# Moving two accumulations of the modulation on the vector engine in a two-block transformer kernel

## The reference, cut to what matters

```python
c_act = jax.nn.silu(c)
mod = (c_act @ w_ada[l] + b_ada[l])[:, None, :]
shift1, scale1, gate1, shift2, scale2, gate2 = jnp.split(mod, 6, axis=-1)
h = rms_norm(x, norm1_w[l]) * (1.0 + scale1) + shift1
proj = h @ w_in[l]
...
A = jnp.where(strict, jnp.einsum('bhncd,bhnsd->bhncs', kb, k) * decay, 0.0)
L = A + jnp.eye(CHUNK, dtype=A.dtype)
sol = lax.linalg.triangular_solve(L, rhs, left_side=True, lower=True, unit_diagonal=True)
qk = jnp.where(causal, jnp.einsum('bhncd,bhnsd->bhncs', q, k) * decay, 0.0)
...
x = x + gate1 * mixed
```

## Time and profile before

| | us |
|---|---|
| median of 3 runs | 953.57 |
| lowest and highest of the runs | 953.0, 954.26 |
| the profiled execution, its own time | 958.16 |
| its span, from the first to the last instruction | 956.1 |
| PE busy in the span | 942.1 (99%) |
| DVE busy | 743.2 (78%) |
| ACT busy | 540.4 (57%) |
| POOL busy | 63.7 (7%) |

### The profile page before, as it was taken

How to read it: one execution, slowest core, us unless ns; L and a number is a source line. 1 busy time by engine, 2 the same in 40 slices (tenths; PEclk the granted TensorE clock), 3 DMA queues, 4 the chain that set the end, 5 groups by cost and what they waited for, 6 DMA issues and landing times.

```text
span 956.1 us, 15251 instructions
## 1 busy us (share of the span) xinstructions
PE 942.1 (99%) x6383; PEld 812.3 (85%) x6383; DVE 743.2 (78%) x841; ACT 540.4 (57%) x687; POOL 63.7 (7%) x60
## 2 busy tenths in 40 slices
PE   8999999999999999999999999999999999999997
PEld 5799888988878788999888888889999888888886
DVE  2699978878887887787669987777776668987874
ACT  3584467466546465634265664657655656655554
POOL 0000660000100000100000000010000000000000
PEclk9999979999999999999999999999999999999999
DMA  9877224766798878556536878778653464978761
GB/s 338 298 255 284 72 84 140 271 219 253 174 354 213 315 182 309 208 181 212 202 115 166 269 214 272 214 212 288 257 170 128 144 218 142 259 217 269 216 176 44
DMA packets 41555, 204.54 MB, mean 214 GB/s; under 512 B 3408, under 2 KB 5904, under 8 KB 25744
## 3 DMA queue, kind: packets, MB, share of 16 engines
q1 hardware_dynamic: 35024, 180.37, 52.0%
q0 software_dynamic: 5760, 22.05, 12.4%
q10 hardware_dynamic: 704, 1.17, 0.4%
HBM read 202.49 MB, written 1.07 MB: 213 GB/s over the span
## 4 chain that ended last, share of the span: by engine, by line
PE 88%; DVE 6%; ACT 2%; DMA 1%; issue 1%; POOL 1%; SPq 0%; DVEq 0%; POOLq 0%; ACTq 0%
PE bank L2179 44%; PE acc L2179 41%; PE bank L2830 2%; DMA X_inv<-stream 1%; DVE w_lo L1419 1%; POOL X_inv L839 1%; PE bank L2576 1%; ACT w_hi L933 0%; DVE scores L1443 0%; DVE XT L1725 0%; PE bank L2281 0%; PE acc L2281 0%; PE bank L2286 0%; PE bank L2453 0%; DVE qkT L1713 0%
## 5 line engine op out<-in xcount | busy, mean ns | idle before, releaser
L1419 DVE TENSOR_TENSOR w_lo<-raw,w_hi 128x2048 fp32r<-128x2048 f32 x125 | 284.5, 2288 | 51.0 <-ACT w_hi L933 50.7
L933 ACT ACTIVATE w_hi<-raw 128x2048 fp32r<-128x2048 f32 x125 | 237.4, 1911 | 66.1 <-PE acc L2179 41.5
L2179 PE MATMUL bank<-w_hi,h_parts 128*128 128x512 f32 x696 | 225.0, 393 | 0.0
L2179 PE MATMUL acc<-h_parts,w_hi 128*128 128x256 f32 x928 | 169.7, 285 | 1.3 <-DVE h_parts L1471 0.7
L2179 PEld LDWEIGHTS bank<-w_hi,h_parts 128*128 128x128 f32 x696 | 130.7, 188 | 29.7 <-DVE h_parts L1496 1.5
L2179 PEld LDWEIGHTS acc<-h_parts,w_hi 128*128 128x128 f32 x928 | 142.3, 188 | 5.7 <-DVE w_lo L1541 2.1
L2179 PE MATMUL bank<-w_lo,h_parts 128*128 128x512 f32 x348 | 135.6, 390 | 0.0
L2179 PE MATMUL acc<-h_parts,w_lo 128*128 128x256 f32 x464 | 130.6, 281 | 0.0
L2179 PE MATMUL acc<-w_hi,o_hi 128*128 128x512 f32 x296 | 117.3, 396 | 1.8 <-DVE w_lo L1419 1.8
L2179 PE MATMUL acc<-w_hi,o_lo 128*128 128x512 f32 x296 | 115.4, 390 | 0.0
L2179 PE MATMUL acc<-w_lo,o_hi 128*128 128x512 f32 x296 | 115.3, 390 | 0.0
(11 more groups left out here) (412 smaller groups left out, 1353.7 us busy)
## 6 DMA issues: line engine op xcount, KB each, us to landing
raw<-stream SPq DMA_DIRECT2D x141, 1024.0 KB, 5.1
t_tables<-stream SPq DMA_DIRECT2D x9, 1024.0 KB, 5.9
x_res<-stream SPq DMA_DIRECT2D x9, 1024.0 KB, 8.1
x_res<-stream POOLq DMA_DIRECT2D x9, 1024.0 KB, 8.7
t_tables<-stream POOLq DMA_DIRECT2D x9, 1024.0 KB, 10.5
raw<-stream SPq DMA_DIRECT2D x6, 512.0 KB, 10.5
AT<-stream SPq DMA_DIRECT2D x2, 1024.0 KB, 11.6
qkT<-stream SPq DMA_DIRECT2D x2, 1024.0 KB, 13.0
```

The source lines that it names most:

```text
L933: act.activation(split_tile((w_hi, w_hi2), w), split_source(w), ACT.Copy).then_inc(s.hi_ready, 1)
L1419: dve.tensor_tensor(split_tile((w_lo, w_lo2), w), split_source(w), split_tile((w_hi, w_hi2), w), ALU.subtract).then_inc(s.lo_ready, 1)
L2179: return pe.matmul(o, l, r, start=start, stop=stop, skip_group_check=True)
```

## The change

`FIRST_BLOCKS` becomes 3, so that the running sum leaves `inv_b` one accumulation earlier. The accumulation between the window heads' statistics and `qkT` goes, and one is added behind the first half of the second softmax's maxima, at level l = 2. Since the accumulations take their blocks in order, block 11 (k = 3) now is done by the statement behind `XT`, which did block 12, and block 12 (k = 4) is done by the new statement at level 2.

```diff
-        mod_acc_first, FIRST_BLOCKS = inv_b[:, :], 4
+        mod_acc_first, FIRST_BLOCKS = inv_b[:, :], 3
...
             dve.reciprocal(ss[:, 1, :], ss[:, 0, :]).then_inc(s.head_inv, 1)
-            accumulate(at)
-            at += 1
             for gi in range(4):
                 wait_big(f"qk{gi}")
...
                 if l == 2:
                     softmax_max(1, A, sc_other, range(2))
+                    accumulate(at)
+                    at += 1
```

## The result

The changed kernel is slower: 958.5 us, the median of 12 runs (955.04 to 960.53), against 954.13 for the kernel before in 12 runs (953.0 to 958.29). The ratio is 1.0035, with a 95% interval of 1.0023 to 1.0048 (the ratio of the medians is 1.0046). The two profiled executions hide this: they take 958.24 and 958.16 us, with spans of 956.4 and 956.1.

The account below looks back on a forecast made before the run. PE was taken to bound the kernel, waiting on DVE between 103 and 124 us. The median 953.57 less 1.86 for the dropped accumulation, with the moved one hidden and loads free, gave 951.7 us; range 947.8 to 953.4.

Parts of the forecast that it names:

- Part 1: One accumulation less ahead of `qkT` on DVE: PE starts level 2 at 122.34 in place of 124.20, gain 1.86 us.
- Part 2, with the fall: Accumulation of 2.34 us at level 2, PE at half clock in levels 2 and 3: hidden with 0.7 us to spare.
- the fall at 125.7: PE's granted clock halves from 2.4 to 1.2 GHz, about 125.7 to 135.9 in the profile before; forecast to stay.
- a rest of 3.06 us: DVE idle behind level 2's maxima, 135.75 to 138.82, until PE lets level 3's update start; meant to hide the accumulation.
- Part 2, at the full clock: Level 2's accumulation runs to 133.55 behind a 0.3 us mask; level 3's update starts there, 134.2 before: gain 0.65 us.
- Part 3: Loads behind weight blocks 11 and 12 are issued later but land before use: no cost, 4.6 us more lateness covered.
- no fall in the timed runs: Rival: timed runs keep the full clock before and after, the accumulation sticks out; gain 0.65 us, 952.9 us, chance 0.25.
- fall as before: The forecast case: half clock at levels 2 and 3 stays, accumulation hidden; gain 1.86 us, 951.7 us, chance 0.30.
- The rival that came true: PE waits about 0.9 us before level 4, clock halves there, levels 4 and 5 pay 4.6 us: 957.5, chance 0.10.
- Faster, same, slower: Chances for the whole kernel: faster (below 951.66 us) 0.43, same 0.47, slower 0.10.

Follow-up runs that it names:

- the run with both accumulations behind the start: The changed kernel with the accumulations of blocks 11 and 12 both behind the start of the inversion, none at level 2: 958.9 us, ratio 1.0048.
- the kernel before with zeros: The kernel before plus 7 matmuls of zeros on PE between the halves of level 1's last products: 953.48 us, ratio 0.9989.
- the first split: The changed kernel with block 12's accumulation in two halves, at levels 2 and 4, POOL's level 4 masks held until the first is done: 957.52 us.
- the run with the zeros: The changed kernel plus 16 matmuls of zeros on PE between the halves of level 3's last products: 953.9 us, ratio 0.9995.
- part 1 alone: The changed kernel with block 12's accumulation at level 2 shrunk to 8 of 2048 columns: 951.95 us, ratio 0.9971.
- part 2 on top: The kernel before plus one 128x2048 instruction at level 2 that adds zero times the running sum: 960.55 us, ratio 1.0059.
- held masks with zeros: The changed kernel with POOL's level 4 masks held until the level 2 accumulation is done, plus 8 matmuls of zeros at level 3: 953.91 us.
- two halves without the late load: The changed kernel, block 12's accumulation halved at level 2 (masks held) and behind level 3's update, plus 7 matmuls of zeros at level 4: 954.14 us.
- the held masks: The changed kernel with POOL's masks of level 4 held until the accumulation at level 2 is done: 954.47 us, ratio 1.0004.

## Why the prediction was wrong, point by point

**Part 1** was right in each step that the trace can test. `qkT` at 105.59 (105.6), the rest of 1.88 us (1.7), `XT` ended at 114.1 (114.15), level 2 started by PE at 122.31 (122.34). The long first `XT` was POOL's doing, and went with it. Alone it is worth 1.9 us within its set (1.7 against all runs of before without a fall), 1.86 by the sum.

**Part 2, with the fall:** the step "with the clock as it was, levels 2 and 3 are PE's" never came to be tested, since the fall at 125.7 didn't come. The claim "It is hidden with 0.7 us to spare" hung on a rest of 3.06 us that only this fall makes. And part 1 itself takes away the wait ahead of the fall: 0.47 us are left of 1.16, and none of the eight traces in which PE waits so little there has a fall at level 2. So the forecast held on to a fall whose likely cause its own first part removed.

**Part 2, at the full clock:** here a term was mis-sized. I worked out that the kernel before would update level 3 at 134.2 without a fall (134.06 measured), and the maxima of the change would be done near 130.9 (131.29). Then I let one mask stand in the way for 0.3 us. In the trace POOL had started its second mask 0.05 us before DVE came, so both masks stood ahead: 1.08 us of standing, the update at 134.57 in place of 133.55. PE's wait is 2.34 us in place of 0.9: 1.0 by the standing, the rest since PE ends level 3's products 0.3 us sooner than summed (133.02). The rows had the two masks without a gap between them, but not which of the engines would ask first: that is as close as 0.05 us. With the first mask running DVE gets in between, as the run with both accumulations behind the start shows. One more term was off: for the rest of DVE without a fall I wrote 1.75 us, where my own terms give 1.4 (134.2 less 130.9 and 1.86) and the kernel before with zeros shows 0.89.

**Part 3:** right for the change: no engine waits for a late load. That the slack is finite, the first split showed.

**The forecast** failed in that step of part 2, the hidden accumulation, and it was chosen because "the fall stands in the only execution that is traced", which was taken as how the kernel runs. The runs show in its place an accumulation of 3.43 us on the path, a wait of PE of 2.34 us behind it and a new fall, 4.6 us by the medians. And the traced execution isn't how the kernel runs. Half of the executions of before have no fall, most others a short one by their mean clock, and the traced one, at 958.16, was 4.6 us over the median and so of the rarest kind. I saw that 4.6 was just the price of the fall, and still gave "no fall in the timed runs" less than "fall as before". All my sums to the median, 953.57 less a gain, mixed two kinds of executions.

**The rival that came true** had 0.10: a new fall ahead of level 4, at 957.5. The place, the waiting engine and the price were right. The run with the zeros gives the price: 958.5 less 953.9, 4.6 us. That this is the price I had put is in part luck: the 12 runs go from 0.997 to 0.991, so some pay less and some more than the one traced. What remains, 953.9 against 953.82 in the same set (953.62 in all), is no gain where I had put 0.65, by the 1.0 us of standing. What I held against it, that PE's work is denser there, doesn't count beside a wait of 2.34 us.

**Faster, same, slower:** 0.90 on "faster" and "same" was wrong, and the upper end of the range, 953.4, lay below even the median of before that was known, 953.57, so that no change at all was outside of it.

What stays open: why a wait of about 1.2 us is followed by a fall in one half of the executions and not in the other. The runs show waits and falls side by side, and no more. By PE's longest wait at these levels in the trace: 0.5 us or less, none of 20 (part 1 alone, zeros in the change); 1.2 to 1.3 us, 36 of 72, 8 of 12 and 6 of 12; 2.3 us and more, 24 of 24 (the change, part 2 on top, both behind the start). Four runs don't fit into this row by length alone: held masks with zeros, 0.6 us, 4 of 12; the kernel before with zeros, 0.73 us, 1 of 11; two halves without the late load, 0.9 us, 3 of 11; the first split, three waits of 0.58, 0.94 and 1.08 us within 7 us, 5 of 5. So the length of the longest wait isn't all that counts. Nor did I trace an execution of before without a fall. The one with zeros stands in for it.

## What to carry to other kernels

Before an operation goes into an engine's idle time, ask what made that time: a rest that exists only while TensorE runs at half its clock is gone as soon as it doesn't, and by then the operation lies on the path. Where two engines exclude each other, look at which one asks first and how many of its instructions follow without a gap; a wait put on the one with slack can undo most of what moving the work has cost. A profiled execution that is far above the median of the timed runs can be another kind of execution, so sums belong to runs of its kind, and each run's mean clock helps to say which kind it is.

## What the runs showed of the hardware that I had not expected

- An instruction of DVE on 8 columns took 1.29 us, and one on 8 values took 0.68 in place of 0.16, while POOL was at work on two inputs in on-chip memory; each ended within 0.02 us of POOL's (132.53 and 132.51, 141.47 and 141.45). The Trainium skill states in "SBUF — State Buffer", section "Who interferes with whom", that a vector instruction with two SBUF inputs contends with a GpSimd instruction that reads SBUF. The trace agrees, and these runs show that even the smallest instruction stands.
- 16 matmuls of zeros, 2.18 us of work that nobody uses, made the changed kernel 4.6 us faster by the medians: with them TensorE's granted clock stayed at 2.4 GHz in 11 of 11 runs.
- A fall isn't always of one length: 10.2 us in the profiled executions of before and after, 6.8 us in that of both accumulations behind the start, about 3.4 us in those of the held masks and of the first split, where mean clocks are 0.997.
